# Transposes on TensorE and up weights of three kept blocks in a diffusion backbone layer (8 cores)

## What is computed

```python
hx = modulate(rmsnorm(x, norm_mix), sh_a, sc_a)            # D_MODEL = 1024
qm, km, vm, om, gates, qa, ka, va = project_tokens(hx, ...) # conv of width 3 + silu on q_m, k_m
hm = mlstm_forward(...) + flip(mlstm_backward(...))         # 4 heads x 128
y_m = mlstm_merge(hm, om, mlstm_norm)
y_a = window_attention(apply_rope(qa), apply_rope(ka), va, ka_c, va_c, sink)  # 8 q heads, 2 kv heads x 64
x = x + g_a * (concat([y_m, y_a]) @ w_out)
a, val = split(modulate(rmsnorm(x, norm_ffn), sh_f, sc_f) @ w_up)             # D_FF = 2816
x = x + g_f * ((gelu(dwconv(a)) * val) @ w_down)
return rmsnorm(x, final_norm)
```

## Time and profile before

| | us |
|---|---|
| median of 3 runs | 1054.87 (1049.04 to 1058.03) |
| profiled execution, its own time | 1058.23 |
| its span, core 3 (the slowest) | 1056.6 |
| spans of the other cores | 1031.1 to 1050.8 |

### The profile page before, as it was taken

The page is one execution under the profiler, slowest core; times in us unless marked ns, Lnnn a source line. Parts: engine busy times, 40 slices in busy tenths (PEclk is TensorE's granted clock), DMA queues, the critical chain, the costliest instruction groups (busy, mean ns, idle before and its releaser), DMA issues.

```text
span 1056.6 us, 18245 instructions; the slowest of 8 cores (1031.1 to 1056.6 us)
## 1 busy us (share of the span) xinstructions
PE 821.1 (78%) x5374; PEld 438.1 (41%) x5374; DVE 645.4 (61%) x1258; ACT 434.7 (41%) x755; POOL 352.9 (33%) x454
## 2 busy tenths in 40 slices
PE   0151669877898964655587499999999999999994
PEld 0130435544444432333343255545554455455551
DVE  0034478778778676653684456555665566667776
ACT  0353634364555653653675334302421144114442
POOL 2133636654311258654462112711221122011111
PEclk9985899989899986868798889999999999999998
DMA  9989998961001177537359999912330034001122
GB/s 140 206 184 214 178 127 71 119 97 21 11 11 17 20 109 112 125 66 130 69 121 143 148 165 166 183 26 46 56 60 16 16 61 70 1 11 62 60 88 112
DMA packets 107790, 96.16 MB, mean 91 GB/s; under 512 B 71728, under 2 KB 88112, under 8 KB 107312
## 3 DMA queue, kind: packets, MB, share of 16 engines
q0 software_dynamic: 30464, 50.37, 33.1%
q1 hardware_dynamic: 77232, 44.64, 19.6%
HBM read 120.77 MB, written 8.39 MB: 122 GB/s over the span
## 4 chain that ended last, share of the span: by engine, by line
PE 59%; DMA 16%; DVE 9%; SPq 6%; issue 6%; ACT 2%; POOL 2%; DVEq 0%; POOLq 0%; ACTq 0%
PE pp L737 38%; PE pp L1780 15%; SPq L241 5%; DMA hxT<-xn 4%; DMA xbuf<-x 3%; DMA wada<-w_ada 3%; DMA hxT<-xnb 2%; PE pp L1285 2%; DMA adst<-w_ada 2%; PE pp L1256 1%; DMA ymT<-ytm 1%; DVE hxT L685 1%; DMA x<-x 1%; PE pp L1163 1%; ACT pT L1261 1%
## 5 line engine op out<-in xcount | busy, mean ns | idle before, releaser
L737 PE MATMUL pp<-hxT,wub 128*128 128x410 bf16 (+3 forms) x1760 | 312.2, 338 | 3.3 <-DMA wub<-w_up 3.3
L737 PEld LDWEIGHTS pp<-hxT,wub 128*128 128x128 bf16 x1760 | 172.3, 98 | 141.9 <-issue 8.0
L1721 ACT ACTIVATE fac<-pp,ffcw 128x410 f32<-128x410 f32 (+1 forms) x110 | 75.5, 688 | 171.7 <-PE pp L737 171.7
L1785 DVE TENSOR_TENSOR x<-pp,x 128x512 f32<-128x512 f32 x128 | 88.5, 692 | 82.2 <-PE pp L1780 82.2
L1780 PE MATMUL pp<-wdb,qT 128*128 128x512 bf16 x384 | 104.8, 382 | 4.7 <-DVE kT L1743 4.6
L1741 ACT ACTIVATE fac<-fac 128x410 f32<-128x410 f32 (+1 forms) x110 | 59.8, 543 | 113.5 <-DVE fac L1736 113.2
L1261 ACT ACTIVATE pT<-pp 128x1024 bf16<-128x1024 f32 x78 | 76.2, 1027 | 43.9 <-PE pp L1256 43.0
L1780 PE MATMUL pp<-wdb,kT 128*128 128x512 bf16 x320 | 90.4, 381 | 0.2 <-PE pp L737 0.2
L737 PE MATMUL pp<-hxT,wq 128*128 128x414 bf16 (+2 forms) x320 | 65.7, 356 | 30.9 <-DVE hxT L685 29.7
L1732 DVE SCALAR_TENSOR_TENSOR fac<-pp,ffcw,fac 128x410 f32<-128x410 f32 (+2 forms) x110 | 70.4, 640 | 24.6 <-ACT fac L1721 22.4
L210 POOL DMA_DIRECT2D wub<-w_up x46 | 25.8, 562 | 170.4 <-PE pp L737 165.8
(11 more groups left out here) (169 smaller groups left out, 1360.7 us busy)
## 6 DMA issues: line engine op xcount, KB each, us to landing
wub<-w_up POOLq DMA_DIRECT2D x46, 512.0 KB, 8.9
xbuf<-x SPq DMA_DIRECT2D x16, 512.0 KB, 9.3
adst<-w_ada POOLq DMA_DIRECT2D x16, 512.0 KB, 11.6
x<-x SPq DMA_DIRECT2D x16, 512.0 KB, 3.9
out<-x SPq DMA_DIRECT2D x16, 512.0 KB, 2.7
wdb<-w_down POOLq DMA_DIRECT2D x22, 256.0 KB, 7.6
wada<-w_ada POOLq DMA_DIRECT2D x8, 512.0 KB, 18.7
wq<-w_qk POOLq DMA_DIRECT2D x8, 256.0 KB, 9.9
```

What stands on the lines that cost most here:

```text
L737: ins = e.matmul(ps1(b)[:, c0:c0 + n], lhs(k), rhs(k), start=(k == 0), stop=(k == KC - 1))
L1721: kb.op("act", lambda e: e.activation(ac[:, 0:m], ps1(ba)[:, o0 - i0:o1 - i0], AF.Identity, bias=ffcw[:, c, 3:4], scale=ffcw[:, c, 1:2]), ...
L1785: kb.op("dve", lambda e: e.tensor_tensor(xs, ps1(b), xs, ALU.add), reads=[PS(b), ("x1_%d" % T, half)], writes=[("x1_%d" % T, half)], dur=t ...
```

## The change

Four things are replaced; the arithmetic is the same.

1. Latent tiles 4 to 15 of the first norm go through `norm_group` in groups of four (`per` = 2 channel blocks to a bank, 4 banks to a group) in place of `norm_dma` and `norm_scale`; pattern `PAT` gives 3 of 8 channel blocks to ACT, 5 to DVE.
2. The rotated keys and queries are transposed on TensorE and copied from PSUM by ACT to `kaT` and `ya`.
3. The backward keys come from `make_ktm` with the copy on ACT; `norm2` is a `norm_group` of two tiles (2 banks a pair; `PAT2` gives 2 of 8 blocks to ACT). `hsq` gets a ring of one.
4. `NPRE` is 3: each of the 22 up blocks is loaded once and serves all five groups; blocks 0 to 2 take part in the early groups.

```diff
@@ kvg_tile
-        yield Req("sp", ["krb%d" % i2])
-        kb.dmat(kaT[:, ti * 128:(ti + 1) * 128].unsqueeze(1), krb[i2][:], reads=["krb%d" % i2], writes=[("kaT", ti)], dur=2.2, issue=0.4)
+        yield Req("pe", ["krb%d" % i2], banks=1)
+        b2 = kb.take()
+        transposes(krb[i2], ["krb%d" % i2], 1, b2)
+        yield Req("act", [PS(b2)])
+        kb.op("act", lambda e: e.copy(kaT[:, ti * 128:(ti + 1) * 128], psb(b2)[:, 0:128]), reads=[PS(b2)], writes=[("kaT", ti)], dur=0.27)
+        kb.give(b2)
@@ qa_tile: the same with 4 transposes of qrb and a 512-wide copy to ya[t]
-    for t0_, n_ in ((0, 2), (2, 2)):
+    for t0_, n_ in ((0, 2), (2, 2), (4, 4), (8, 4), (12, 4)):
         sig.append((-0.8, norm_group([NCT + t0_ + i for i in range(n_)], xnof, R_xnb, hxT, t0_ * 128,
                                     [("hxT", t0_ + i) for i in range(n_)], 0, 1, PAT)))
-    for t0_, n_ in ((4, 2), (6, 2), (8, 4), (12, 4)):
-        for i in range(n_):
-            sig.append((-1.0, norm_dma(t0_ + i)))
-        sig.append((-0.8, norm_scale(t0_, n_)))
@@ back_kt
-            for h in range(4):
-                kb.dmat(bufof[kk][:, h:h + 1, :], kT[:, h, T * 128:(T + 1) * 128], reads=qkeys("kT", T), writes=[(kk, h)], dur=2.2, issue=0.35)
+            yield from make_ktm(T + NCT, kk, "act")
@@ norm2 (norm2_dma is gone)
+        yield from norm_group([NTT + T, NTT + T + 1], bufof, R_xn, hxT, T * 128, [("hxT", T), ("hxT", T + 1)], 4, 5, PAT2, xn2_of)
@@ up order
-    NPRE = NGT
-    loads = [(c, [g]) for g in (4, 3, 2) for c in range(NPRE)] + [(c, [1, 0]) for c in range(NPRE)]
-    loads += [(c, list(range(NG))) for c in range(NPRE, NCG)]
-    up = [(n, g) for n, (c, gs) in enumerate(loads) if c < GROUPS[-1][0] for g in gs]
-    up += [(n, g) for g in range(NG) for n, (c, gs) in enumerate(loads) if c >= GROUPS[-1][0]]
+    NPRE = 3
+    loads = [(c, list(range(NG))) for c in range(NCG)]
+    up = [(c, g) for g in range(NG - 1, -1, -1) for c in range(NPRE)]
+    up += [(c, g) for c in range(NPRE, GROUPS[-1][0]) for g in range(NG)]
+    up += [(c, g) for g in range(NG) for c in range(GROUPS[-1][0], NCG)]
@@ load_down
-            yield Req("pool", rings=[R_wdb], when=lambda: m_done() and min(3 * NPRE + 2 + c, len(loads) - 1) in wub_of)
+            yield Req("pool", rings=[R_wdb], when=lambda: m_done() and min(2 + c, NCG - 1) in wub_of)
```

More of the change, by code:

```diff
@@ L669, in norm_bank @@
         kb.give(b)
[L671 to L686, removed]
     def HX(t):
@@ L784, in qa_tile @@
         kb.give(b)
-        yield Req("sp", ["qrb%d" % i2])
-        kb.dmat(ya[t][:], qrb[i2][:], reads=["qrb%d" % i2], writes=["ya%d" % t])
+        yield Req("pe", ["qrb%d" % i2], banks=1)
+        b2 = kb.take()
+        transposes(qrb[i2], ["qrb%d" % i2], 4, b2)
+        yield Req("act", [PS(b2)])
+        kb.op("act", lambda e: e.copy(ya[t][:], psb(b2)[:, 0:512].rearrange("p (g t) -> p g t", g=4)), reads=[PS(b2)], writes=["ya%d" % t], dur=0.6)
+        kb.give(b2)
         kb.made.add(("qa", t))
@@ L1154, in pairv, with state_mm @@
         return ps2(b).rearrange("p (b x) -> p b x", b=2)[:, :, 0:w]
-    def state_mm(ti, d_, kk, vk, kkeys=None):
+    def state_mm(ti, d_, kk, vk):
         b = kb.take(2)
@@ L1164, in mm @@
             return ins
-        kb.op("pe", mm, reads=(kkeys or [kk]) + [vk], writes=[PS(b), PS(b + 1)], dur=t_pe(129, 4))
+        kb.op("pe", mm, reads=[kk, vk], writes=[PS(b), PS(b + 1)], dur=t_pe(129, 4))
         return b
@@ L1356, in build @@
     R_cb = Ring(["Cbx"])
+    R_hq = Ring(["hsq"])
     def more_m():
@@ L1410, in back_kt @@
         for T in range(NT - 1, 0, -1):
-            yield Req("sp", rings=[R_ktb], when=m_ready)
-            yield Req("sp", qkeys("kT", T), rings=[R_ktb])
+            yield Req("pe", banks=1, rings=[R_ktb], when=m_ready)
+            yield Req("pe", qkeys("kT", T), banks=1, rings=[R_ktb])
             kk = R_ktb.take()
-            for h in range(4):
-                kb.dmat(bufof[kk][:, h:h + 1, :], kT[:, h, T * 128:(T + 1) * 128], reads=qkeys("kT", T), writes=[(kk, h)], dur=2.2, issue=0.35)
+            yield from make_ktm(T + NCT, kk, "act")
             kk_of[T] = kk
@@ L1427, in back_step @@
         vb = vb_of[T]
-        kkeys = [(kk, h) for h in range(4)]
-        yield Req("pe", kkeys + [vb], banks=2)
-        b2 = state_mm(ti, 1, kk, vb, kkeys)
+        yield Req("pe", [kk, vb], banks=2)
+        b2 = state_mm(ti, 1, kk, vb)
         R_ktb.give(kk)
@@ L1496, in mlstm_tile @@
         HK = [(hsk, h) for h in range(4)]
-        yield Req("act", HK)
+        yield Req("act", HK, rings=[R_hq])
+        R_hq.take()
         kb.op("act", lambda e: e.activation(hsq[:], hs[:], AF.Square, scale=float(1.0 / np.sqrt(128.0))), reads=HK, writes=["hsq"], dur=0.63)
@@ L1502, in mlstm_tile @@
         kb.op("dve", lambda e: e.tensor_reduce(ss, hsq[:], AX.X, ALU.add), reads=["hsq"], writes=[("fsm", fi, 2)], dur=t_dve(512))
+        R_hq.give("hsq")
         yield Req("pool", HK + ["og%d" % T])
@@ L1564, in build @@
     PAT2 = ["dve", "dve", "act", "dve", "dve", "act", "dve", "dve"]
[L1566 to L1572, removed]
-    def norm2(T):
[L1575 to L1588, removed]
+    def norm2(T):
+        yield from norm_group([NTT + T, NTT + T + 1], bufof, R_xn, hxT, T * 128, [("hxT", T), ("hxT", T + 1)], 4, 5, PAT2, xn2_of)
         kb.made.update([("H2", T), ("H2", T + 1)])
@@ L1598, in build @@
         st.append((0.0, norm2(T)))
-    for T in range(NT - 1, -1, -1):
-        st.append((0.0, norm2_dma(T)))
     NGT = 8
```

## The result

| | before | after |
|---|---|---|
| median of 4 runs, us | 1055.71 | 1019.77 (1017.96 to 1021.01) |
| ratio of after to before | | 0.9667, interval 0.9627 to 0.9707 |
| profiled execution, its own time, us | 1058.23 | 1017.96 |
| its slowest core, span in us | core 3, 1056.6 | core 4, 1016.4 |

The change made the kernel 35 us faster by the ratio. The ratios leave out executions in which the cores of one die ran at a lower clock. 989 was forecast; the range of 945 to 1032 holds 1019.8, but the gain is only 54% of the 66 us.

What follows compares the result with a forecast made beforehand. Stage 4 was taken as bound by TensorE, with time to be had at 50 to 165 and 375 to 614 us, where DMA transposes led the waits. Terms -22 - 47 + 3 = -66 gave 989 us, range 945 to 1032.

Steps and rivals of the forecast that it cites:

- Term 1: First norm and rotated tiles (stage 1) off DMA transposes: -22 us, range -5 to -40.
- of these 256 us: TensorE's work from 50 to 375 us, 242.2 us plus 14 for added transposes; 52 to 61 done before 122 us.
- rival (d): Slower: 77 transpose groups wait in TensorE's in-order list, deciding from 0.86 us each; at 1.2 us, 1081 us; chance 0.05.
- Rival (c): DMA transposes cost the engines no more than plain transfers; stage 1 gives only -6, total 1005 us; chance 0.06.
- the bound of part 1: Stage 1's DMA engine limit: after removing transposes priced at 38 us, the rest needs 81 us, to 131 at latest.
- Term 2: Stage 3, key and hxT transposes taken off SP's queue: -47 us, range -15 to -75.
- Sum 48: Stage 3's gain by its chain: 31 us of hxT landings plus 17, half of SP's issuing.
- The check by engines: Stage 3 by TensorE's work at the best stretch's 80%: 195 us, 44 less; at DMA-independent DVE rate 164, 75 less.
- Term 3: Up weights loaded once, three blocks kept: +3 us, range 0 to +9; saved loads worth nothing in stage 4.
- The stall that the +3 stood for: After stage 3's last tile, 8.2 us of remaining pieces against block 3's 8.9 us load: 0 to 9 us, taken as 3.
- Rival (a): Everything comes: TensorE finds work through stage 1, stage 3 runs at DVE's best rate; -110, 945 us; chance 0.18.
- Rival (b): Little comes: stage 1 waits for modulation weights, stage 3 for merge lanes; -5 - 20 + 5, 1035 us; chance 0.14.

Runs made afterwards that it cites:

- rate125: Changed kernel, its planner counting on the slow early DMA rate until its 125th us instead of its 50th; 1007.9 us, ratio 0.9544.
- stage3_dma: Changed kernel with stage 3's transposes (backward keys and second norm) back on DMA; 1049.4 us, ratio 0.9927.
- up_old: Changed kernel with the old order of the up weights (46 loads, 8 blocks offered to groups 4, 3, 2); 1031.7 us, ratio 0.974.
- before_upnew: Kernel before with only the new order of the up weights (22 loads, three kept blocks), all transposes still by DMA; 1043.9 us, ratio 0.9868.
- stage1_dma: Changed kernel with the transposes of stages 1 and 2 (norm tiles 4 to 15, rotated keys and queries) back on DMA; 1015.0 us, ratio 0.9608.
- kt_dma: Changed kernel with only the backward keys back on DMA (60 transposes on SP's queue); 1024.1 us, ratio 0.9693.
- s1dma_rate125: Changed kernel with the transposes of stages 1 and 2 back on DMA and the planner's slow early rate until the 125th us; 1026.8 us, ratio 0.972.
- n2_dma: Changed kernel with only the second norm back on DMA (16 transposes); 1032.3 us, ratio 0.977.

## Why the prediction was right, and where it was not

**The bound and the side: right.** Stage 4 stayed TensorE's (427.6 against 426.5 us), most of the gain came in stage 3, its hxT landings and SP issuing left the chain, and the granted clock of that stage rose to 0.87 of a foretold 0.9.

**Term 1, -22 us: wrong as a saving, 8 us by the landmark and nothing in the whole.** Its first half held: ACT began to write the last tile's bf16 form at 117.8 us instead of 138.7 (medians), and core 4's last norm transposes started at 130 us; 122 had been taken for a full hxT, 110 to 131 as bounds. The step that failed is "of these 256 us it does 52 ... to 61 before 122 us". TensorE did 30.7 by 125 us, because the lists of ACT and TensorE were written for tiles that come faster than they do. I had given rival (d) 0.05 for the whole kernel and put against it that "the planner puts them where it expects their inputs". That is just what it does, and its expectation (300 KB per us from the 50th us on) was wrong. So rival (d) had the mechanism, and not the size: TensorE's idle time before L645 and L1125 (L1138 of the kernel before) has a median of 55 us over the cores, 61 on core 4, where "over 60" was to be the sign of (d); 15 of them stood there before the change. That is about 0.5 us for each of its 77 groups, less than the 0.86 from which it decides. It also left out the evictions on ACT, which the prediction had called hidden by ACT's idle time. An engine's idle time hides nothing that stands behind a wait in its list. rate125 shows that the order was the cause: 51.2 us of work, and 13 us of the whole. What stage 1's transposes are worth in the best order of each kind stays open: 7 us, within the intervals.

The price of the transposes on the DMA engines was right. SP's queue took 66 us of the engines for 13.14 MB from 50 to 165 us. After the change (core 4) it takes 23.8% of 115, 27 us, for 8.57 MB, all of them plain loads:

```profile
q1 hardware_dynamic: 2926, 8.57, 23.8%
```

That is 3.2 us per MB. At this price the 7.6 MB of plain loads before took 24 us, which leaves 42 us for the 5.5 MB of transposes, an estimate; 38 had been taken, between 28 and 47. The Trainium skill's rule ("Advanced Engine Details and Errata", section "X-Bar Transpose (TRN2)"), that transpose DMAs are as fast as regular ones, is not borne out here: 42 us for 5.5 MB are 7.6 us per MB against 3.2. Rival (c), which is this rule, came near with its -6 for term 1 all the same, and that was luck; its "15 us early" is also not what the bound of part 1 gives with its numbers, 50 + 105 = 155 us against 156.

**Term 2, -47 us: the mechanism was right, the size was not, 27 us.** The step that failed is "Sum 48", an addition. Of the chain's entries I counted the hxT landings at 31 us and half of the issuing at 17. Taken out of stage3_dma one at a time they are 25 and 17 us, close to what was said of each, but together 27: whoever removes one has removed most of the other's price. Shares of one chain were added as if the next path lay far behind; it lay close. Part of the closeness is luck, since stage3_dma pays 12 us at the last landing that the kernel before hardly paid. The check by engines used the share of the best 25 us (TensorE 80%) for all of stage 3. It reached 75%: on core 4, 16.8 and 12.4 us of the first two 25 us, and 21.0 to 21.5 of each 25 from 469 to 544 us. The start stands around the end of attention, whose place hardly moved; that attention bounds it is a reading.

**Term 3, +3 us: wrong side, -8 to -14 us.** The failing sentence is "The 24 loads saved are worth nothing in stage 4", read from one window after the shortage was over. In up_old the first 50 us of stage 4 ran at the pace of the loads. The stall that the +3 stood for did not come: TensorE was busy 50 of the first 50 us. The fear of the missing filling was idle: in before_upnew three kept blocks ran 192 up matmuls against 176. That the changed kernel had only 138 comes from the order its planner found, as the 136 to 192 of the kernels here show; what in the planner decides it stays open.

The parts can be added one after the other, by the ratios: the up weights on the kernel before 14 us (before_upnew), then stage 3's transposes 27 (stage1_dma), then stage 1's -6 (the changed kernel): 35, which is what was measured. By the landmarks 28 us of it lie in stage 3 and 8 in stages 1 and 2. The runs put it otherwise: more than a third of the 35 is the up weights, and nothing is stage 1's transposes. Against term by term, terms 1 and 2 were 28 and 20 us too large and term 3 had the wrong sign by 17; that they partly cancel is luck, and the total is off by 31 only. Rival (a) failed with stage 1. Rival (b) foretold a stage 3 gain of 20, near the 27, but its reason for stage 1 was wrong: the modulation weights' last matmul moved from 218.4 (after) to 192.2 us (rate125) by order alone.

## What to carry to other kernels

When a transfer becomes an instruction on an engine that runs its list in order, what the scheduler believes about the arrival of its input becomes part of its price: compare planned and measured arrival before counting a saving, and look, on the engine that evicts as well as on the one that computes, for a wait with ready work behind it. And price two changes in the same order that you mean to keep: one line of the planner was worth 13 us to one kernel and cost its twin 12. Price shares of a chain from both sides, by removing them one at a time and together: here each alone brought 25 and 17 us of a pair worth 27, and each put back alone cost 11 and 3. Look at the longest landing beside the median. Last, read a load's bandwidth in the first windows after a hand-over, not in the middle of the steady part.

## What was not expected of the hardware

SP's queue issuing 60 key transposes at about 1.1 us each costs 3 us in all when the second norm is elsewhere (kt_dma), though it is 10.3% of the chain. The DMA engines' share in the first 75 us was 1.17 with transposes beside loads (s1dma_rate125, median of the cores) against 0.98 without (rate125), for nearly the same rate, 191 and 187 GB/s. And the same transpose of 256 KB that lands in 3.2 us in the median took 16.9 us (median of the cores, n2_dma) when it was issued among seven weight loads.
